# Two query units side by side, value pages half a unit earlier in the order, and 96 products of zeros ahead of the first tokens

## What is computed

```python
proj = x @ w_in_l                                   # prompt_mixer, sample_mixer: 2048 -> 7184 columns
q, k, v, beta, g = dn_prep(short_conv(x_pad, conv_w), proj[..., OFF_BA:OFF_AA], proj[..., OFF_AA:OFF_QB], a_log, dt_bias)
oa, S = gated_delta_chunked(q, k, v, beta, g)       # samples: gated_delta_recurrent
oa = gated_rmsnorm(oa, proj[..., OFF_ZA:OFF_BA], norm_w)
ob = moba_prompt(qb, kbl, vbl, kmean, rel_bias)     # samples: moba_attend over paged keys and values
x = post_norm(x, merge_groups(oa, ob, w_out_l), ln_g[0], ln_b[0])
x = post_norm(x, cross_attend(x, mk, mv, w_q, w_o), ln_g[1], ln_b[1])
x = post_norm(x, swiglu(x, w1, w2), ln_g[2], ln_b[2])
```

## Time and profile before

| | us |
|---|---|
| median of 3 runs | 1602.91 |
| lowest, highest | 1602.39, 1605.07 |
| the profiled execution's own time | 1602.35 |
| its span, first to last instruction | 1600.4 |
| PE busy | 1540.7 |
| DVE busy | 932.9 |
| ACT busy | 644.2 |
| POOL busy | 182.7 |

### The profile page before, as it was taken

How to read it: one execution, slowest core, us unless ns; L and a number is a source line. 1 busy time by engine, 2 the same in 40 slices (tenths; PEclk the granted TensorE clock), 3 DMA queues, 4 the chain that set the end, 5 groups by cost and what they waited for, 6 DMA issues and landing times.

```text
span 1600.4 us, 36185 instructions
## 1 busy us (share of the span) xinstructions
PE 1540.7 (96%) x14680; PEld 1495.3 (93%) x14680; DVE 932.9 (58%) x1130; ACT 644.2 (40%) x752; POOL 182.7 (11%) x286
## 2 busy tenths in 40 slices
PE   7999999999998879999999999999999999999996
PEld 6999999999898779997899999999999999999995
DVE  4445645557753345774487666666666644445566
ACT  5344333343523443464454333544333333333344
POOL 0000202021577510001000000000011000000000
PEclk9999999999999999999999999999999999999998
DMA  8698878886788977455645545555677655555453
GB/s 308 218 338 338 314 282 331 290 319 219 222 250 259 288 281 309 172 184 200 244 163 183 172 171 183 185 180 187 241 261 255 214 185 183 184 183 174 165 179 113
DMA packets 104339, 365.17 MB, mean 228 GB/s; under 512 B 14385, under 2 KB 48378, under 8 KB 77210
## 3 DMA queue, kind: packets, MB, share of 16 engines
q1 hardware_dynamic: 89682, 322.66, 58.0%
q0 software_dynamic: 12752, 39.73, 7.2%
q10 hardware_dynamic: 1792, 1.20, 0.4%
HBM read 353.27 MB, written 10.47 MB: 227 GB/s over the span
## 4 chain that ended last, share of the span: by engine, by line
PE 76%; issue 8%; ACT 5%; DVE 5%; DMA 4%; SPq 2%; POOLq 1%; POOL 1%; ACTq 0%; DVEq 0%
PE psum_g L519 21%; PE psum_g L520 21%; PE psum_g L521 21%; PE M L2122 3%; PE M L2137 3%; DVE wl L503 2%; ACT wh L498 2%; DMA raw<-w_in_t 1%; PE M L519 1%; PE psum_g L2431 1%; PE M L520 1%; PE M L521 1%; DMA sraw<-cache_k_t 1%; SPq L630 1%; ACT xf L1124 1%
## 5 line engine op out<-in xcount | busy, mean ns | idle before, releaser
L519 PE MATMUL psum_g<-xh,wh 128*128 128x264 f32 (+1 forms) x2414 | 709.0, 294 | 24.0 <-DVE wl L503 11.9
L520 PE MATMUL psum_g<-xl,wh 128*128 128x264 f32 (+1 forms) x2414 | 688.8, 285 | 0.0
L521 PE MATMUL psum_g<-xh,wl 128*128 128x264 f32 (+1 forms) x2414 | 687.9, 285 | 0.0
L503 DVE TENSOR_TENSOR wl<-raw,wh 128x2048 fp32r<-128x2048 f32 (+1 forms) x223 | 502.6, 2254 | 310.6 <-ACT wh L498 310.1
L498 ACT CAST wh<-raw 128x2048 fp32r<-128x2048 f32 (+1 forms) x223 | 418.2, 1875 | 248.9 <-PE psum_g L521 204.4
L519 PEld LDWEIGHTS psum_g<-xh,wh 128*128 128x128 f32 x2414 | 458.6, 190 | 40.3 <-issue 23.1
L520 PEld LDWEIGHTS psum_g<-xl,wh 128*128 128x128 f32 x2414 | 458.8, 190 | 3.1 <-issue 2.9
L521 PEld LDWEIGHTS psum_g<-xh,wl 128*128 128x128 f32 x2414 | 457.0, 189 | 0.0
L519 PE MATMUL psum_g<-gh,wh 128*128 128x264 f32 x704 | 200.4, 285 | 0.2 <-DVE wl L503 0.2
L521 PE MATMUL psum_g<-gh,wl 128*128 128x264 f32 x704 | 199.4, 283 | 0.0
L520 PE MATMUL psum_g<-gl,wh 128*128 128x264 f32 x704 | 199.4, 283 | 0.0
(11 more groups left out here) (431 smaller groups left out, 1698.6 us busy)
## 6 DMA issues: line engine op xcount, KB each, us to landing
raw<-w_t SPq DMA_DIRECT2D x88, 1024.0 KB, 4.9
raw<-w_in_t SPq DMA_DIRECT2D x55, 1024.0 KB, 7.8
kring<-cache_k_t SPq DMA_DIRECT2D x96, 512.0 KB, 4.6
sraw<-cache_k_t SPq DMA_DIRECT2D x32, 512.0 KB, 6.1
raw<-w_out_t SPq DMA_DIRECT2D x16, 1024.0 KB, 5.1
raw<-w2a_t SPq DMA_DIRECT2D x16, 1024.0 KB, 4.8
raw<-w2b_t SPq DMA_DIRECT2D x16, 1024.0 KB, 4.9
raw<-w2c_t SPq DMA_DIRECT2D x16, 768.0 KB, 4.2
```

Of the source, the lines that this page charges most:

```text
L503: eng.tensor_tensor(wl[:, u % 2, 0:nk], raw[:, u % 2, 0:nk], wh[:, u % 2, 0:nk].bitcast(F32), ALU.subtract).then_inc(raw_used, 1)
L519: nc.tensor.matmul(out, hi_w, x_hi(k), start=(k == order[0]), stop=False)
L520: nc.tensor.matmul(out, hi_w, x_lo(k), start=False, stop=False)
L521: last = nc.tensor.matmul(out, lo_w, x_hi(k), start=False, stop=(k == order[-1]))
```

## The change

Six parts.

1. Unit 1 also comes in quarters, and PE multiplies quarter by quarter, unit 0's and then unit 1's. Unit 2 comes in quarters too, each when unit 0's low quarter is made, and is split in halves for ACT and DVE. The gates' products stand behind unit 1. Of the constants only the identity comes ahead of unit 3, the rest behind it. The page keys start one unit later. ACT makes the high part of unit 4 ahead of the sigmoid and its table loads.
2. Before all this PE waits for `ab0`, a memset, and multiplies that tile of zeros, 128 x 48, by itself 96 times in float32.
3. From group 3 on, each value group stands half a unit earlier on PE. `spread` stays where it is. POOL issues its loads of group 0 ahead of `decays(3)`, and stores the first half of `kv` ahead of them, the second where all of it went.
4. At the end of stage b DVE makes the last gated head and `oz` ahead of the last quarter `lo3` of the attention half.
5. In stage out ACT's table load stands behind the high part of unit 1.
6. The first norm has six parts, with the high and low part of xq's unit 1 before its last two; the last norm has the same six parts (2, 2, 4, 4, 2, 2 chunks) in place of 4, 4, 4, 2, 2.

```diff
         def groups_at(u, end):
 
-            group = 2 * (u - KEY_UNITS - 3) + end - 1
-            return (group,) if 0 <= group < 16 else ()
+            first = 2 * (u - KEY_UNITS - 3)
+            groups = {(0, 1): (0,), (2, 0): (1,), (2, 1): (2, 3)}.get((first, end), (first + end,) if first > 2 else ())
+            return tuple(g for g in groups if g < 16)
...
             pool.wait_ge(k_used, K_RING + NSAMP * PAGES)
             nc.gpsimd.memset(zp_flat, 0.0).then_inc(e_pool.sem, 1)
-            decays(3)
+            pool.wait_ge(psum_free, 4 * turn + KEY_UNITS + 2)
+            pool.dma_start(o["kv"][:, 0:8], kv[:, 0:8]).then_inc(e_out, 16)
             pool.wait_ge(pid_back, 16)
             values(0)
+            decays(3)
             values(1)
...
             turn, n = STAGES["q"]
-            pe.wait_ge(psum_free, 1)
+            wait(pe, s_pool, "ab0")
+            zeros = ab.rearrange("p c n -> p (c n)")
+            for _ in range(96):
+                nc.tensor.matmul(M[0:48, 1, 0:48], zeros, zeros, start=True, stop=True)
+            pe.wait_ge(psum_free, 2)
...
-            products(pe, psum_g[:, 0, 0:T], 0, lambda w, s, k: w[:, s, k], XH, XL, KC, before=quarter, done=mm_done)
+            for g in range(PARTS):
+                for s in range(2):
+                    wait(pe, s_dve, f"l{'wv'[s]}{g}")
+                    for k in range(per * g, per * (g + 1)):
+                        out, end = psum_g[:, s, 0:T], k == KC - 1
+                        nc.tensor.matmul(out, wh[:, s, k], xh[:, k], start=(k == 0), stop=False)
+                        nc.tensor.matmul(out, wh[:, s, k], xl[:, k], start=False, stop=False)
+                        last = nc.tensor.matmul(out, wl[:, s, k], xh[:, k], start=False, stop=end)
+                        if end:
+                            last.then_inc(mm_done, 1)
...
             for g in (2, 3, 0, 1):
-                if g == 0:
+                if g == 3:
                     gated(H - 1)
...
             turn, n = STAGES["out"]
-            act.preload_act_table_set("natural_log_exp_and_others")
             for i in range(n):
                 for u in range(4):
                     upper_next(act, turn + i, u)
+                    if i == 0 and u == 0:
+                        act.preload_act_table_set("natural_log_exp_and_others")
```

More of the change, by code:

```diff
@@ L355, in build @@
         d_const, d_tabs, d_small, d_ab = (sem(n) for n in ("d_const", "d_tabs", "d_small", "d_ab"))
[L356 removed]
+        d_x = [sem(f"d_x{g}") for g in range(PARTS)]
+        d_w, d_v, d_y = ([sem(f"{n}{g}") for g in range(PARTS - 1)] for n in ("d_w", "d_v", "d_y"))
+        d_eye = sem("d_eye")
         d_mem, mem_out = sem("d_mem"), sem("mem_out")
@@ L612, in _ @@
             sp.wait_ge(raw_used, 1)
-            for g in range(PARTS):
-                part = slice(per * g, per * (g + 1))
+            parts = [slice(per * g, per * (g + 1)) for g in range(PARTS)]
+            first, second, third = (w_tile(a["w_in_t"], KTAIL + u) for u in range(3))
+            for g, part in enumerate(parts):
+                end = g == PARTS - 1
                 sp.dma_start(x_in[:, part], a["x_t"][:, part]).then_inc(d_x[g], 16)
[L616 to L619, removed]
+                sp.dma_start(raw[:, 0, part], first[:, part]).then_inc(raw_full[0] if end else d_w[g], 16)
+                sp.dma_start(raw[:, 1, part], second[:, part]).then_inc(raw_full[1] if end else d_v[g], 16)
+            for g, part in enumerate(parts):
+                wait(sp, s_dve, f"lw{g}")
+                sp.dma_start(raw[:, 0, part], third[:, part]).then_inc(raw_full[0] if g == PARTS - 1 else d_y[g], 16)
+            sp.dma_start(C[:, 0:P], a["constants"][:, 0:P]).then_inc(d_eye, 16)
+            load_unit(sp, turn, 3, w_tile(a["w_in_t"], KTAIL + 3))
+            sp.dma_start(C[:, P:], a["constants"][:, P:]).then_inc(d_const, 16)
             sp.dma_start(conv_w[:].rearrange("p j c -> p (j c)"), a["conv_w_t"]).then_inc(d_tabs, 16)
@@ L636, in load_pages @@
                       .then_inc(k_full[m % K_RING], 16)
-            for u in range(2, 4 * n):
+            for u in range(4, 4 * n):
                 load_unit(sp, turn + u // 4, u % 4, w_tile(a["w_in_t"], KTAIL + u))
-                if 3 <= u < 7:
-                    half = u - 3
-                    load_pages(half // 2, range(2 * (half % 2), 2 * (half % 2) + 2))
+                half = u - 4
+                load_pages(half // 2, range(2 * (half % 2), 2 * (half % 2) + 2))
             turn, n = STAGES["a"]
@@ L736, in _ @@
                         load_unit(sp, i + turn, u, w_tile(a[s2_ + "_t"], i * 4 + u), nk)
-            for g, part in enumerate(Y_PARTS):
+            for g, part in enumerate(LN_PARTS):
                 sp.wait_ge(y_ready, g + 1)
@@ L1118, in layer_norm @@
                 nc.scalar.activation(rstd[:], rstd[:], ACT.Exp, scale=-0.5).then_inc(l_act.sem, 1)
-                for g, part in enumerate(ln_parts(i)):
+                for g, part in enumerate(LN_PARTS):
                     if g in before:
@@ L1776, in layer_norm @@
                     at("n3")
-                    centre(4)
-                    scale(4)
-                else:
-                    centre(2)
-                    low(0)
-                    scale(2)
-                    low(1)
-                    for g in (3, 4):
+                    for g in (4, 5):
                         centre(g)
                         scale(g)
-                    low(2)
-                low(3)
-                low(4)
+                    low(3)
+                    at("n5")
+                    low(4)
+                    low(5)
+                else:
+                    for g in range(2, NG):
+                        centre(g)
+                        scale(g)
             wait(dve, f_dve, "lo1")
@@ L2085, in _ @@
             last.then_inc(s_pe.sem, 1)
-            unit(pe, turn, 1, XH, XL)
+            wait(pe, s_dve, "l2")
+            pe.wait_ge(psum_free, 3)
+            products(pe, psum_g[:, 0, 0:T], 0, lambda w, s, k: w[:, s, k], XH, XL, KC,
+                     before=lambda k: pe.wait_ge(raw_used, 5) if k == 2 * per else None, done=mm_done)
             wait(pe, s_act, "abt")
```

82 lines of the change are left out of this document (46 added, 36 removed).

## The result

The changed kernel is slower: a median of 1616.62 us over 9 runs, against 1604.53 of the kernel before over 9 runs taken beside them. The ratio is 1.0072, with a 95% interval of 1.0058 to 1.0086, so 11.6 us, between 9.3 and 13.8. Some 4 us of them belong to these two executions and not to the change.

The account below looks back on a forecast made before the run. PE's waits outside the long feed-forward stretch, and the low clock behind them, were taken as what can move. 5.0 + 3.3 + 2.0 - 8.5 = 1.8 us gained, giving 1600.6 us; range 1593 to 1607.

Parts of the forecast that it names:

- Start: Start and stage q: zeros end at 11.8, unit 4 ends at 43.3 in place of 48.3; 5.0 us gained.
- Rival E: Units 2 to 5 come late because keys and constants share the DMAs; start's gain shrinks to about 2, 1603.6 us; chance 0.07.
- POOL's later `decays(3)` costs nothing: Stage b, POOL: by its issue times it ends about 2 us before PE asks for it; no cost.
- Value pages: Units 37 to 42: PE waits 18.4 us on the spread, 12.1 of page waits vanish, low clock adds; 8.5 us lost.
- the 2.5 expected back at unit 46: ACT's 2.28 us wait for unit 46's weights goes; with what lay ahead of it, 2.5 us comes back.
- Stage out: Passage into stage out: unit 1's high part sooner, low-clock stretch gone; 3.3 us gained, between 2.1 and 3.7.
- First norm: xq's unit 1 no longer waits 1.38 for its low part, unit 0's wait shortens; 2.0 us gained, 1.4 to 2.2.
- last norm: Final norm: ACT starts 1.65 sooner but then waits for DVE; 0 gained, within 0.3.
- A: Cheap zeros, 0.030 a record, end before the tokens come; only three long waits lower the clock; 1596.2 us; chance 0.27.
- B: The spread doesn't hold PE; the half unit gains some 1.5 in place of 8.5 lost; 1590.6 us; chance 0.08.
- C: Dear zeros, 0.07 a record, ending at 17.1; the start gains -0.3; 1605.9 us; chance 0.10.
- D: Zeros don't raise the clock, which stays low until tokens come; start loses 3.7, in all 6.9; 1607.5 us; chance 0.08.

Follow-up runs that it names:

- experiment 4: Changed kernel with SP reading the list of key pages into registers once for two half bursts, not for each; 1615.47 us, ratio 1.0055 to the kernel before.
- experiment 14: Changed kernel with value groups at old places, `decays(3)` between group 0's two heads, all key-page lists read ahead of unit 2's quarters; 1598.87 us, 0.9963 to the kernel before.
- experiment 8: Kernel before with parts 1 and 2 alone (two units side by side, zeros); 1605.76 us, ratio 1.0008 to the kernel before.
- experiment 15: Changed kernel without parts 1 and 2, value groups at old places, `decays(3)` between group 0's two heads; 1598.49 us, ratio 0.9965 to the kernel before.
- experiment 7: Kernel before with part 3 alone (half-unit order of value groups, POOL's order, `kv` in halves); 1616.55 us, ratio 1.0078 to the kernel before.
- experiment 6: Kernel before with POOL's order alone: first half of `kv` stored and group 0's loads issued ahead of `decays(3)`; 1601.68 us, ratio 0.9985.
- Experiment 3: Changed kernel with POOL's `decays(3)` back ahead of the first value-page loads; 1623.87 us, ratio 1.0108 to the kernel before.
- experiment 10: Changed kernel with parts 4 and 5 undone (table load ahead of out's unit 1, `oz` behind `lo3`); 1619.27 us, ratio 1.0097 to the kernel before.
- experiment 1: Changed kernel with the value groups back at their old places on PE; 1602.07 us, ratio 0.9976 to the kernel before.
- experiment 2: Changed kernel with DVE copying the spread ahead of its delta step, readout and low part, half-unit order kept; 1599.06 us, 0.9959 to the kernel before.
- experiment 5: Changed kernel without the 96 products of zeros; 1615.69 us, ratio 1.0064 to the kernel before.

## Why the prediction was wrong

It had 1.8 us gained; the two profiles are 15.8 apart the other way, 17.6 more. The terms, in their order:

**Start, 5.0 gained.** The working up to unit 4 was right: E 11.67 for 11.8, a zero's record every 0.080 at first and 0.046 later (29 records from 1.75 to 4, 49 from 7.80 to 10) against my 0.088 and 0.044, unit 4's end 43.9 for 43.3. The step that failed is the sentence "with E the end of the zeros and all later waits hidden", carried past unit 4. A gain at unit 4 is a gain at the end only if nothing behind it is paced by something else. SP's reads paced the loads of units 5 to 8 (experiments 4 and 14), and key pages the bursts behind them (read from the waits in experiment 8). In the profile pair 4.4 of the 5.0 were missing by unit 12. Rival E named the loads, but for another reason and at 3 us.

**Stage a, nothing forecast.** 6.1 lost. 3.3 are waits for key pages (4.2 for 0.9). How much of that is the start's doing is open: these waits come to 0.9, 1.2, 2.3 and 3.1 in the four kernels with the old start (before, experiments 15, 7 and 6), and to between 1.6 and 5.1 in the thirteen with the new one. The other 3.0 or so are the second failed step, "POOL's later `decays(3)` costs nothing". I had only asked whether PE gets it in time, not what runs beside it: 1.25 on the low part and 1.7 of clock behind the longer wait. Experiment 3 showed both by taking them away, though it lost more by the later page loads. The clock's part is not certain: in experiments 7 and 10 the low part took 3.61 and 3.63 and PE waited 2.32 and 2.33, and no stretch at the low level followed.

**Value pages, 8.5 lost.** The mechanism and the sum of waits were right to the tenth: 18.4. The 12.1 vanished as said, though experiments 1 and 6 show that POOL's seven microseconds, not PE's lateness, did most of it. The clock was mis-sized: 8.5 less 1.7 instead of 6.0 less 1.3, since one wait of 4.20 was followed by 6.8 us at the lower level. And the 2.5 expected back at unit 46 did not come: PE is 18.5 us behind at unit 45 and 18.6 at unit 47. ACT's wait for these weights did go, but it was not what held PE there: before, PE had no wait for unit 46's low part, only one of 1.68 for DVE's chain at 571.15. 18.4 - 12.1 + 6.8 = 13.1, 4.6 more than forecast. That this meets the table to the tenth is partly luck: it leaves out smaller waits (3.7 against 2.1 before), and PE stood idle for 1.1 of the 17.0 us at the lower level. With experiment 2 the cause is shown: the spread moved, nothing else, and the loss was gone.

**Stage out, 3.3 gained.** 2.2 had come by out's unit 2 (18.6 behind at unit 47, 16.4 there); 1.4 went back to late weights. The profile pair has 0.9 left of the 3.3, experiment 10 puts the net at 4.0, uncertain by 3.6; how much the term was off stays open.

**First norm 2.0, last norm 0.** 1.9 and 0.

The rivals: A, B, C and D were about the price of the zeros and about whether the spread holds PE, and both came out as in the forecast. None had the place where the time went. The slower side was given to a clock that does not rise on zeros, while the loss came from a term already written down and taken too small, a start whose gain was not followed past unit 4, and an edit costed at nothing. D's time was added up wrongly besides: 6.9 us lost on 1602.35 is 1609.3, not 1607.5 (it was added to the forecast, which has the other terms in it already), and slower then begins where the start loses 0.6, not 1.4. The range of 1593 to 1607 was made from the zeros' price, the best known part; with D's right time its upper end would still have been below 1616.6.

## What to carry to other kernels

When a consumer is moved up in one engine's order, move its producer too: here one 0.2 us copy, standing behind 4.3 us of other work of its engine that it doesn't need (2.3 of it the low part), cost 15 us, and putting it first gave 18 back. A gain at the head of a pipeline has to be followed through the next queue that paces it, register reads of the issuing engine included. And an instruction moved to another time "costs nothing" only if the engine it now runs beside was looked at as well as the one that waits for it.

## What the runs showed of the hardware

**VectorE and GpSimd hold each other up.** In ten kernels `decays(3)`, a product whose two operands both lie in SBUF, began 0.32 to 0.50 us after a low part, a subtraction of that kind. In seven, with 0.32 to 0.43 between the starts, DVE's took 3.54 to 3.64 for 2.29 and POOL's 1.05. In three, with 0.48 to 0.50, it was the other way about, as in experiment 1:

```profile
413.47 2.29 DVE L501 TENSOR_TENSOR wl<-raw,wh 128x2048 fp32r<-128x2048 f32 x1 [2.20 <-ACT wh L496]
415.68 1.26 DVE L1414 SCALAR_TENSOR_TENSOR pj<-kv 128x256 f32<-128x256 f32 x1
...
413.97 2.69 POOL L778 TENSOR_TENSOR chain<-C,g_hc 128x512 f32<-128x512 f32 x1
```

POOL's took 2.69 for 1.05 and ended 0.9 us behind the low part, and DVE's next instruction, beside that end, took 1.26 for 0.42. In these traces one waits out the other whole; they don't share. What decides which of the two waits is not shown beyond the distance of their starts. The Trainium skill, "Advanced Engine Details and Errata", section "GPSIMD Details", says that the two share a read and a write interface, which conflicts where VectorE's instruction has two SBUF inputs. These traces agree, with the 1.25 us beside it.

**GpSimd's issue rate is a resource.** A page costs it 0.58 us (2.33 for four). A group of 12 with its pauses takes 8.0 us (their first pages go out at 444.7, 452.7, 460.6 and 468.6 in the changed kernel), against 7.9 of PE's time in the kernel before (spreads at 455.3, 471.4 and 486.9, two groups each). Experiment 6's 8.3 and 0.59 were a little high. At rates so close it doesn't catch up once it is behind; started seven microseconds sooner, it stays ahead for most of the stage.

**SyncE's register reads.** One list of four numbers took 5.7 to 6.3 us in the changed kernel and 4.8 to 6.6 in experiment 8, beside the loads; the two lists of experiment 14, read one behind the other, took 6.4 together (7.54 to 13.96; the quarter of VectorE's that the next issue also waits for was done at 8.3). The profile has no row for them; they appear as a gap between two issues.

**PEclk at the start.** The windows of the first 5 us show 1.00 although the records of the zeros run at half pace until about 5.4, and in experiment 5 so does the window from 8.5 to 13.5, in which the products are 0.22 apart; the column does not show this first stretch. Where it ends differs from run to run: the zeros end at 11.67 in the changed kernel, at 12.4 in experiment 8.
